# A first weight block loaded in quarters, a table scaled on another engine, and multiplications of constants in TensorE's waits

## What is computed

```
for layer in range(4):
    h = rmsnorm(x, attn_norm[layer])
    m = mixer(h, w_qkv, rel_bias)        # layer 0: diff_attention, with bias_tab[t5_bucket(dist)]
    x = x + m @ w_o[layer]
    x = x + conv_gated_ffn(rmsnorm(x, ffn_norm[layer]), ...)
x = rmsnorm(x, final_norm)               # then: ffn1, moba attention + pool, cross attention
x = x + rmsnorm_2(c, xa_post_g)          # c: cross attention's output projection
x = x + 0.5 * rmsnorm_2(swiglu(rmsnorm_2(x, ffn2_pre_g), w_gate, w_up, w_down), ffn2_post_g)
```

## Time and profile before

| | |
|---|---|
| median of 3 runs | 1781.01 us (1780.96 to 1781.06) |
| the profiled execution | 1781.53 us, of which the span from first to last instruction is 1779.8 us |
| TensorE busy | 1755.8 us, 99% of the span |
| VectorE, ScalarE, GpSimd busy | 71%, 57%, 5% |
| 16 DMA engines | mean 172 GB/s |

### The profile page before, as it was taken

The page is one execution under the profiler, slowest core; times in us unless marked ns, Lnnn a source line. Parts: engine busy times, 40 slices in busy tenths (PEclk is TensorE's granted clock), DMA queues, the critical chain, the costliest instruction groups (busy, mean ns, idle before and its releaser), DMA issues.

```text
span 1779.8 us, 35522 instructions
## 1 busy us (share of the span) xinstructions
PE 1755.8 (99%) x14256; PEld 1710.6 (96%) x14256; DVE 1256.6 (71%) x1827; ACT 1007.0 (57%) x1504; POOL 87.4 (5%) x138
## 2 busy tenths in 40 slices
PE   8999999999999999999999999999999999989998
PEld 7999999989999998999999999999999999989997
DVE  7668868877787886787876677788555776565555
ACT  5676555656655566655566755566443655364343
POOL 2000000022000013000000000003000020000000
PEclk9999999999999999999999999999999999999999
DMA  9444655534565545565554456555555554536552
GB/s 288 153 148 153 208 183 159 190 129 132 166 213 177 175 162 161 166 212 178 170 186 143 143 181 199 187 176 193 190 183 175 168 164 139 167 123 196 180 179 92
DMA packets 238423, 306.34 MB, mean 172 GB/s; under 512 B 13698, under 2 KB 212916, under 8 KB 238268
## 3 DMA queue, kind: packets, MB, share of 16 engines
q1 hardware_dynamic: 236692, 300.27, 52.2%
q0 software_dynamic: 1504, 4.28, 0.7%
q10 hardware_dynamic: 104, 0.07, 0.0%
HBM read 303.53 MB, written 1.07 MB: 171 GB/s over the span
## 4 chain that ended last, share of the span: by engine, by line
PE 90%; DVE 4%; ACT 3%; DMA 1%; issue 1%; POOL 0%; DVEq 0%; ACTq 0%; POOLq 0%
PE ps L1029 28%; PE ps L1030 28%; PE ps L1031 28%; PE ps L1194 1%; ACT sb_w_hi L858 1%; DVE sb_w_lo L1574 1%; DMA sb_bias<-bias_dram 1%; PE ps L1214 1%; DMA sb_raw<-in_da_w_qkv 0%; PE ps L1244 0%; PE ps L1231 0%; PE ps L1186 0%; DVE sb_a_hl L1588 0%; PE ps L1311 0%; PE ps L1042 0%
## 5 line engine op out<-in xcount | busy, mean ns | idle before, releaser
L1029 PE MATMUL ps<-sb_a_hl,sb_w_hi 128*128 128x256 f32 x3120 | 892.4, 286 | 8.0 <-ACT sb_a_hl L905 3.1
L1030 PE MATMUL ps<-sb_a_hl,sb_w_hi 128*128 128x256 f32 x3120 | 883.3, 283 | 0.0
L1031 PE MATMUL ps<-sb_a_hl,sb_w_lo 128*128 128x256 f32 x3120 | 883.2, 283 | 0.0
L1574 DVE TENSOR_TENSOR sb_w_lo<-sb_raw,sb_w_hi 128x2048 fp32r<-128x2048 f32 x283 | 646.7, 2291 | 327.4 <-ACT sb_w_hi L858 327.0
L858 ACT ACTIVATE sb_w_hi<-sb_raw 128x2048 fp32r<-128x2048 f32 x283 | 538.3, 1906 | 239.7 <-PE ps L1031 230.2
L1029 PEld LDWEIGHTS ps<-sb_a_hl,sb_w_hi 128*128 128x128 f32 x3120 | 598.5, 192 | 18.4 <-issue 10.0
L1030 PEld LDWEIGHTS ps<-sb_a_hl,sb_w_hi 128*128 128x128 f32 x3120 | 598.6, 192 | 0.8
L1031 PEld LDWEIGHTS ps<-sb_a_hl,sb_w_lo 128*128 128x128 f32 x3120 | 598.7, 192 | 0.0
L1029 PE MATMUL ps<-sb_hh,sb_w_hi 128*128 128x256 f32 x912 | 257.1, 282 | 0.0
L1030 PE MATMUL ps<-sb_hl,sb_w_hi 128*128 128x256 f32 x912 | 256.8, 282 | 0.0
L1031 PE MATMUL ps<-sb_hh,sb_w_lo 128*128 128x256 f32 x912 | 256.6, 281 | 0.0
(11 more groups left out here) (251 smaller groups left out, 1443.0 us busy)
## 6 DMA issues: line engine op xcount, KB each, us to landing
sb_raw<-in_ffn_w_up SPq DMA_DIRECT2D x102, 1024.0 KB, 5.4
sb_raw<-in_ffn_w_down SPq DMA_DIRECT2D x66, 1024.0 KB, 4.9
sb_raw<-in_da_w_qkv SPq DMA_DIRECT2D x24, 1024.0 KB, 6.0
sb_raw<-in_ffn_w_gate SPq DMA_DIRECT2D x22, 1024.0 KB, 5.3
sb_raw<-in_w_o SPq DMA_DIRECT2D x16, 1024.0 KB, 5.0
sb_raw<-in_sb_w_qkv SPq DMA_DIRECT2D x12, 1024.0 KB, 5.2
sb_raw<-in_xa_wkv SPq DMA_DIRECT2D x8, 1024.0 KB, 5.4
sb_raw<-in_w_in SPq DMA_DIRECT2D x8, 1024.0 KB, 5.6
```

What stands on the lines that cost most here:

```text
L1029: pe.matmul(o, hi1, hi2, start=start, stop=False, skip_group_check=True)
L1030: pe.matmul(o, hi1, lo2, start=False, stop=False, skip_group_check=True)
L1031: return pe.matmul(o, lo1, hi2, start=False, stop=stop, skip_group_check=True)
L1574: dve.tensor_tensor(w_lo[:, a % RING, :], raw[:, a % RING, :], w_hi[:, a % RING, :].bitcast(F32), ALU.subtract).then_inc(lo_ready, 1)
```

## The change

- Block 0 is loaded by two DMAs of 512 KB, chunks 0 to 3 with a semaphore of their own. ScalarE and VectorE make its first half in two quarters (128x512 each); TensorE waits for a quarter at chunk 0 and at chunk 2.
- ScalarE asks for the exp/ln table set at its very start. Its new order: pair 0, quarter 0, quarter 1, the scaling of the bias table (taken over from VectorE), pairs 1 and 2, second half of block 0, pair 3, `split(1)`, squares.
- VectorE's new order: x pairs 0 and 1, low pair 0, quarter 0, x pair 2, quarter 1, low pair 1, x pair 3, second half, low pairs 2 and 3, `split(1)`, sum of squares.
- TensorE multiplies `ones` by `ident` into a spare bank (`keep_warm`): three times before the first gains, six before x, six after the bias table, twelve after `square_total_of_four`.
- Into the last FFN, `split(n+2)` stands in front of the squares on ScalarE and in front of the sum of squares on VectorE.

```diff
                         src = io[w][l][:, c0:c0 + BW].rearrange("(k p) n -> p k n", p=P)
+                        if ph["n"] + i == 0:
+                            sp.dma_start(slot(0, KC)[:, 0:4, :], src[:, 0:4, :]).then_inc(s_half_block, 16)
+                            load(0, 0, slot(0, KC)[:, 4:8, :], src[:, 4:8, :])
+                            continue
...
+            exp_and_ln(act)
             act.wait_ge(s_gain, 1)
             prep_hi(phases[0], 0)
+            act.wait_ge(s_half_block, 16)
+            for i in range(2):
+                es = slice(i * BE // 4, (i + 1) * BE // 4)
+                act.activation(w_hi[:, 0, es], raw[:, 0, es], ACT.Copy).then_inc(first_hi, 1)
+            act.wait_ge(s_setup_pe, 6)
+            act.activation(table_sb, UB[1][0:16, 0:TW], ACT.Copy, scale=ROOT_HD).then_inc(s_tab, 1)
             prep_hi(phases[0], 1)
+            prep_hi(phases[0], 2)
             act.wait_ge(raw_ready[0], 16)
-            act.activation(w_hi[:, 0, 0:BE // 2], raw[:, 0, 0:BE // 2], ACT.Copy).then_inc(first_hi, 1)
             act.activation(w_hi[:, 0, BE // 2:], raw[:, 0, BE // 2:], ACT.Copy).then_inc(hi_ready, 1)
-            prep_hi(phases[0], 2)
             prep_hi(phases[0], 3)
+            split(1)
             for i in range(4):
                 square_pair(x[:, 2 * i:2 * i + 2, :], i)
-            split(1)
...
+                    if not ph["blocks"]:
+                        split(ph["n"] + 2)
                     for i in range(4):
                         square_pair(x[:, 2 * i:2 * i + 2, :], i)
...
-                        if s0 == 0:
+                        if s0 == 0 and ph["dst"] != "tok":
                             split(b + 2)
...
                 if not ph["blocks"]:
-                    return square_total_of_four(ph)
+                    square_total_of_four(ph)
+                    keep_warm((ph["u"] + 3) % 4, 12)
+                    return
...
-                            if ph["n"] == 0 and k == 0:
-                                pe.wait_ge(first_lo, 1)
+                            if ph["n"] == 0 and k in (0, 2):
+                                pe.wait_ge(first_lo, k // 2 + 1)
...
+            def keep_warm(bank, n):
+
+                for _ in range(n):
+                    pe.matmul(UB[bank][:, 0:P], ones[:, :], ident[:, :], start=True, stop=True, skip_group_check=True)
+
             pe.wait_ge(s_const, 2)
+            keep_warm(3, 3)
             pe.wait_ge(s_first, 16)
...
             ins.then_inc(s_setup_pe, 1)
+            keep_warm(3, 6)
             pe.wait_ge(s_xin, 16)
...
                 .then_inc(s_setup_pe, 1)
+            keep_warm(3, 6)
...
+                if ph["src"] == "y" and not ph["blocks"]:
+                    split(ph["n"] + 2)
...
+            take_x(0)
+            take_x(1)
             dve.wait_ge(s_gain, 1)
             lo_pair(phases[0], x, 0)
+            first_quarter(0)
+            take_x(2)
+            first_quarter(1)
             lo_pair(phases[0], x, 1)
+            take_x(3)
             dve.wait_ge(hi_ready, 1)
...
-            dve.wait_ge(s_setup_pe, 6)
-            dve.tensor_scalar(table_sb, UB[1][0:16, 0:TW], ROOT_HD, None, ALU.mult).then_inc(s_tab, 1)
```

More of the change, by code:

```diff
@@ L282, in model_kernel @@
         s_poolw = sem("s_poolw")
+        s_half_block = sem("s_half_block")
         first_hi = sem("first_hi")
@@ L2079, in _, with take_x, first_quarter @@
                 .then_inc(s_gain, 1)
-            for i in range(4):
+            def take_x(i):
                 dve.wait_ge(s_setup_pe, i + 2)
                 dve.tensor_copy(x[:, 2 * i:2 * i + 2, :], pairs(DB[i])).then_inc(x_ready, 1)
+            def first_quarter(i):
+                es = slice(i * BE // 4, (i + 1) * BE // 4)
+                dve.wait_ge(first_hi, i + 1)
+                dve.tensor_tensor(w_lo[:, 0, es], raw[:, 0, es], w_hi[:, 0, es].bitcast(F32), ALU.subtract)\
+                    .then_inc(first_lo, 1)
+            take_x(0)
+            take_x(1)
             dve.wait_ge(s_gain, 1)
             lo_pair(phases[0], x, 0)
-            dve.wait_ge(first_hi, 1)
-            dve.tensor_tensor(w_lo[:, 0, 0:BE // 2], raw[:, 0, 0:BE // 2], w_hi[:, 0, 0:BE // 2].bitcast(F32), ALU.subtract)\
-                .then_inc(first_lo, 1)
+            first_quarter(0)
+            take_x(2)
+            first_quarter(1)
             lo_pair(phases[0], x, 1)
+            take_x(3)
             dve.wait_ge(hi_ready, 1)
```

## The result

The changed kernel takes 1784.76 us (median of 17 runs, 1783.8 to 1785.91), the kernel before 1781.01 (17 runs, 1780.5 to 1782.04): a ratio of 1.0018, with an interval of 1.0012 to 1.0025. It is slower by 3.75 us, which is at the edge of the 0.2% up to which I had called it the same (the interval has 1.002 in it), outside the predicted range of 1778.6 to 1783.4, and 2.1 us from the predicted 1782.7. Its profiled execution took 1785.32 us, span 1783.6; against the 1779.8 of before that is +3.8.

The account below looks back on a forecast made before the run. The prediction took the bias chain to set the time up to 40 us. Opening 0, clock +1.5, last-FFN constants 0 and order +0.25 summed to +1.75 us: 1782.7 us on the median, range 1778.6 to 1783.4.

Parts of the forecast that it names:

- What bounds the kernel: Up to 40 us the chain of block 3's load, bias load, mask and maxima sets the time, 0.9 us over TensorE.
- The bias chain: Opening: the earlier table buys nothing; `scores(1)` starts at 40.37 us as before, opening 0.
- The queue beside it is filled as before: 12.5 us again.: Opening: the bias load takes 12.5 us as before, its neighbouring queue being filled the same.
- Rival 4: Opening: blocks asked for earlier cut the bias load's share; `scores(1)` moves by 4.3 us, total 1785.6; chance 0.03.
- Block 3: Opening: issued 0.8 us earlier, its load lands no sooner behind the sinks; no gain, bounds 0 and -0.8 us.
- First product: Opening: TensorE's first product comes at 10.5 us instead of 13.20; TensorE's lead is 2.5 us.
- the last six constants by then too: Opening: TensorE's last six constants are done by 10.2 us, ahead of a first product at 10.5.
- The clock: In front of `scores(1)`: 3.4 us of idling drops the clock to half, +1.5 us, bounds 0 and 1.5.
- Last FFN: Constants cost 0, bounds 0 and +2.0 us; the new order delays the sum of squares, +0.25, bounds -1.45 and +0.5.
- Rival 1: The clock stays up at 40 us: +0.25 us, total 1781.3; chance 0.22.
- rival 2: Opening: block 3 and the bias land up to 0.8 us earlier, total 1780.5, or 1782.0 with a clock fall; chance 0.17.
- rival 3: Opening: bias chain 2.5 us earlier, lead kept, total 1778.7, or 1777.0 if the last FFN saves 1.45; chance 0.08.

Follow-up runs that it names:

- Run 7: The change with its first bias load in two DMAs of eight heads, first maxima waiting for the first half only: 1778.92 us, ratio 0.9986.
- run 4: The change with block 5's load held back until block 3's low part is made: 1780.09 us, ratio 0.9994.
- run 5: The change with block 5's load held back and eight constants ahead of the wait of `scores(1)`: 1781.07 us, ratio 0.9996.
- run 6: The change without the opening's fifteen constants: 1784.09 us, ratio 1.0016.
- run 1: The change with fifteen more constants in front of the wait of `scores(1)`: 1782.57 us, ratio 1.0009.
- run 2: The change without GpSimd's wait for block 3 before the bias load: 1784.72 us, ratio 1.0016.
- run 3: Two kernels: the last-FFN part alone put into the kernel before, 1782.01 us; the change without its last-FFN part, 1784.7 us.
- run 8: Bias in halves, four kernels: kernel before 1781.25 us; change without last-FFN part 1778.84, without opening's constants 1779.09, with first block whole 1779.39.

## Why the prediction was wrong

**What bounds the kernel: right.** The bias chain set the time to 40 us, and what was gained on the table bought nothing. Its write was issued 5.7 us earlier (11.70 against 17.36) and landed 3.4 earlier, at 19.8, since it took 8.1 us and not 5.8; the forecast had it near 16. Run 7 shows the chain's hold by removing it.

**The bias chain: the step that failed.** "The queue beside it is filled as before: 12.5 us again." It took 13.33. The sentence in front of it had the cause, that blocks 4 and 5 are asked for some 2 us earlier, and then I looked at the queue at 30 us, where the load has its full share beside blocks 5 and 6, and not at 25 to 28 us, where the load begins. Rival 4 named the mechanism but had it as a loss of share for the whole load, at 4.3 us; it was a late start, at 0.84 (q0's first packets 3.75 us behind the issue instead of 2.9). The Trainium skill ("DMA: Bandwidth & Descriptors", section on queues, rings and completion order) has each DMA engine take turns between its rings. That agrees with the stretch in which both queues flow, 75 packets against 72 in before. For the 3 us in which q0 has no row, the trace doesn't tell whether its packets were there to be taken; where q1 had run dry (runs 4 and 5) they came 1.7 us behind the issue, and in after q1 alone flowed for 2 us more. The bounds failed as well: for block 3 I took 0 and -0.8, for the load none, and both went the other way, by 0.40 and 0.84. I bounded an unknown from the side on which I expected a gain.

**Block 3: right in kind.** As forecast, the sinks ahead of it set its landing and its issue did not (run 6): they landed 0.3 us later than before, and block 3 0.4. The issue itself came at 15.24 and not at 14.3: ScalarE waited for TensorE's table product until 10.9 us, before it could make pairs 1 and 2 and then the second half of block 0.

**First product: 10.5 forecast, 12.18 measured.** The step that failed is "the last six constants by then too". I had added up ScalarE's and VectorE's work, and not TensorE's own list: turns from 6.99 to 10.1 (in part at half rate, the case that I had set aside), then the table's 0.8, then constants from 10.82 on. Quarter 0's low part was there at 11.0. Most of the miss is the turns: in eight traces with this opening (after, runs 1, 2, 4, 5 and 7, and one each of runs 3 and 8) they take 2.19 to 3.56 us, and in every one the first product comes 9.02 or 9.03 us plus their length into the span. With the forecast's half of 3.67 that would be 10.9. So the lead was 1.6 us in after's trace, not 2.5. It changed nothing in the result, since the lead went into the wait anyway: 0.92 + 1.6 + 1.24 = 3.76.

**The clock: right, a term mis-sized.** It fell where forecast. I took 3.4 us of half rate and 1.5 lost, and 1.5 as the upper bound; it was 6.8 us and 2.43 (2.2 by run 1). Of the 6.8, 5.44 were worked. I had taken the length of the stretch before as the most that it could be. 1.5 is what two other traces lost (runs 3 and 6), so the number was not absurd, but as a bound it failed.

**Last FFN: right.** Constants 0. Order +0.08 instead of +0.25: the sum of squares waited until 1598.96, which, less the 3.66 us by which the row of eight is late, is the 1595.3 of the forecast; the next product followed it by 0.35 instead of 0.5.

**The sum.** Forecast 0 + 1.5 + 0 + 0.25 = 1.75; measured in the traces 1.24 + 2.43 + 0 + 0.08 = 3.75; the two traced executions differ by 3.79 and the medians by 3.75. That the medians agree to the hundredth is chance: the half rate alone cost 1.5 in some executions and 2.4 in others. Rival 1 (clock stays up) falls by the clock row, rival 2 by block 3's landing, rival 3 by the chain; each had a part of the chances that the term which decided, a slower bias load, should have had.

## What to carry to other kernels

When an edit makes an engine faster that isn't on the chain, list the transfers that it will ask for earlier, and look at what the queues carry in the stretch in which the chain's own transfer starts; here one that was issued while the other queue filled the engines came 0.84 us late, with its share later unchanged. Time gained ahead of a wait turns into idling, and idling can cost a second time through TensorE's clock: fix the wait first (here by loading the part that is needed first on its own), and the same gain of 2.3 us is kept. Bound an unknown cost on both sides, and read the timeline of every engine's own list before saying when its first useful instruction comes.

## What the runs showed of the hardware that I had not expected

- From 25 to 28 us GpSimd's load of 2 MB, issued at 24.75, had no packet in the records while SP's queue moved 1.04 MB; in the execution in which SP's queue moved 0.06, it moved 0.54. Its first packets came 1.7 to 3.8 us behind its issue.
- In a wait of 3.76 us the granted clock fell at 40.25 us and stood at half for 6.8 us, though TensorE worked in 5.44 of them. After 3.29 us it stayed full (run 2). After 2.51 us it stayed full in one kernel (hold of block 5) and was at 0.68 from 41 to 44 us, behind the start of `scores(1)`, in another (no constants). After the same 3.1 us at the last FFN it stayed full in before and fell in three kernels without constants there (0.57 to 0.69 over some 4 us).
- The granted clock's column reads 1.00 from the start of a trace to about 13 us, even where TensorE's steps are those of half rate (x's turns, 0.23 us each). Over the same turns some executions pass to 0.12 us a turn and others later or not at all, which moves the first product by up to 1.4 us.
- Block 3 landed between 23.4 and 24.4 us for issues between 14.6 and 15.6, one of the latest issues having the earliest landing; it came 2.5 to 2.9 us behind the landing of the sinks each time.
